# Gated DeltaNet layer on one core: when the output weight tiles are rounded in the even units

## The reference

```
h = rms_norm(x, norm_w) * (1 + scale) + shift            # scale, shift, gate from silu(c) @ ada_w + ada_b
p = h @ w_in                                             # 1024 x (q 1024, k 1024, v 2048, z 2048, b 8, a 8)
q, k, v = silu(causal_short_conv(q|k|v, conv_w))         # 4 taps
q, k = l2_norm(q) * 128**-0.5, l2_norm(k)
o = gated_delta_rule_chunked(q, k, v, sigmoid(b), g)     # 8 heads, key width 128, value width 256
o = rms_norm(o, norm_w) * silu(z)
x = x + gate * (o @ w_out)
out = rms_norm(x, final_norm_w)
```

## Time and profile before

| | us |
|---|---|
| median of 3 runs | 1266.35 |
| lowest and highest | 1266.05, 1270.23 |
| the profiled execution | 1268.89 |
| span of the profiled execution | 1267.1 |
| PE busy in the span | 1130.3 (89%) |
| DVE busy | 852.0 (67%) |
| POOL busy | 583.8 (46%) |
| ACT busy | 453.1 (36%) |

### The profile page before, as it was taken

The page is one execution under the profiler, slowest core; times in us unless marked ns, Lnnn a source line. Parts: engine busy times, 40 slices in busy tenths (PEclk is TensorE's granted clock), DMA queues, the critical chain, the costliest instruction groups (busy, mean ns, idle before and its releaser), DMA issues.

```text
span 1267.1 us, 19510 instructions
## 1 busy us (share of the span) xinstructions
PE 1130.3 (89%) x5628; PEld 921.6 (73%) x5628; DVE 852.0 (67%) x1896; ACT 453.1 (36%) x1038; POOL 583.8 (46%) x817
## 2 busy tenths in 40 slices
PE   2787699998999989998999989998999989998985
PEld 1665478777787878777787868877787868877763
DVE  3746668585857767585857767585758767585845
ACT  3452233424333332424333342434333432434323
POOL 3114454447444644447344644446344644446413
PEclk9888699999999999999999999999999999999988
DMA  9522331222222231222222231223122131213002
GB/s 302 168 84 76 89 92 38 61 55 67 63 51 51 62 76 38 59 54 76 54 49 52 63 76 38 60 53 84 45 59 54 50 76 45 66 40 92 21 34 117
DMA packets 150754, 88.31 MB, mean 70 GB/s; under 512 B 29446, under 2 KB 145320, under 8 KB 150696
## 3 DMA queue, kind: packets, MB, share of 16 engines
q1 hardware_dynamic: 150696, 87.73, 25.4%
HBM read 78.28 MB, written 9.44 MB: 69 GB/s over the span
## 4 chain that ended last, share of the span: by engine, by line
PE 54%; DVE 13%; POOL 13%; issue 13%; ACT 2%; DMA 2%; SPq 1%; DVEq 1%; POOLq 0%; ACTq 0%
PE bank L401 24%; PE bank L499 14%; POOL w_lo L1317 6%; DVE work L912 4%; POOL wo_lo L1324 3%; DVE y L945 3%; PE bank L545 2%; POOL w_raw L1331 2%; PE bank L459 2%; DMA work<-in_ada_w 2%; DVE gate_bc L1155 1%; PE bank L555 1%; PE bank L558 1%; PE bank L468 1%; PE bank L475 1%
## 5 line engine op out<-in xcount | busy, mean ns | idle before, releaser
L1317 POOL TENSOR_TENSOR w_lo<-w_raw,w_hi 128x256 fp32r<-128x256 f32 x384 | 316.8, 855 | 319.3 <-ACT w_hi L673 319.1
L401 PE MATMUL bank<-h_hi,w_hi 128*128 128x512 f32 x760 | 315.5, 415 | 28.7 <-POOL w_lo L1317 28.7
L401 PE MATMUL bank<-h_hi,w_lo 128*128 128x512 f32 x760 | 311.5, 410 | 0.0
L401 PE MATMUL bank<-h_lo,w_hi 128*128 128x512 f32 x760 | 310.5, 409 | 0.0
L401 PEld LDWEIGHTS bank<-h_hi,w_hi 128*128 128x128 f32 x760 | 144.9, 191 | 60.7 <-POOL w_lo L1317 33.1
L912 DVE SCALAR_TENSOR_TENSOR work<-pre,cw,work 128x512 f32<-128x512 f32 x192 | 173.1, 902 | 15.4 <-DVE work L909 5.4
L401 PEld LDWEIGHTS bank<-h_hi,w_lo 128*128 128x128 f32 x760 | 144.5, 190 | 30.2 <-issue 0.2
L401 PEld LDWEIGHTS bank<-h_lo,w_hi 128*128 128x128 f32 x760 | 144.8, 191 | 28.6
L1367 POOL TENSOR_TENSOR og_lo<-work,og_hi 128x256 fp32r<-128x256 f32 x64 | 47.1, 736 | 223.6 <-ACT og_hi L733 223.6
L699 ACT ACTIVATE work<-work 128x512 f32<-128x512 f32 x64 | 40.5, 633 | 300.3 <-DVE pre L920 143.2
L499 PE MATMUL bank<-wo_hi,og_hi 128*128 128x512 f32 x256 | 113.1, 442 | 16.3 <-DVE y L945 16.3
(11 more groups left out here) (174 smaller groups left out, 1897.3 us busy)
## 6 DMA issues: line engine op xcount, KB each, us to landing
w_raw<-in_gdn_w_in SPq DMA_DIRECT2D x96, 512.0 KB, 4.0
work<-in_ada_w SPq DMA_DIRECT2D x8, 1024.0 KB, 9.3
w_raw<-in_gdn_w_out SPq DMA_DIRECT2D x16, 512.0 KB, 3.3
y<-in_x SPq DMA_DIRECT2D x8, 512.0 KB, 8.1
work<-in_ada_w SPq DMA_DIRECT2D x8, 512.0 KB, 5.1
n_dram<-work SPq DMA_DIRECT2D x16, 256.0 KB, 4.5
out<-y SPq DMA_DIRECT2D x8, 512.0 KB, 2.7
t_dram<-work SPq DMA_DIRECT2D x16, 64.0 KB, 1.6
```

Of the source, the lines that this page charges most:

```text
L401: mm = nc.tensor.matmul(bank[m % 2][:, :], w[:, m % 2, k, :], h[:, k, half, :], start=(r == 0), stop=(r == MM - 1))
L1317: i = nc.gpsimd.tensor_tensor(w_lo[:, k % 2, j:j + 2, :], w_raw_k[:, k % 2, j:j + 2, :], w_hi[:, k % 2, j:j + 2, :].bitcast(F32), ALU.subt ...
```

## The change

In even units that have an output tile to prepare, three things change places. On ACT, the rounding of output tile 0 goes ahead of the tanh of k, and the rounding of output tile 1 goes ahead of the read-out of z (tile 1) and of the rounding of stream tile 3. On POOL, the low half of output tile 1 goes ahead of that of stream tile 3. No instruction is added or removed, and no wait.

```diff
@@ ACT, body(), not last @@
                     evacuate(u, 0)
                     split_hi(u, hd, par, 2)
-                    tanh(u, 0, 0, cvk[:, other, :])
                     if par == 0:
                         split_wo(hd, 0, u)
+                    tanh(u, 0, 0, cvk[:, other, :])
                     square(u + 1, "k", bank[6], k_ss)
                     decay_exp(u + 1)
+                    if par == 0:
+                        split_wo(hd, 1, u)
                     evacuate_z(u, 1, 0)
                     split_hi(u, hd, par, 3)
-                    if par == 0:
-                        split_wo(hd, 1, u)
@@ POOL, body(), not last @@
                     norm_k(u + 1)
                     mask_decay(u + 1)
-                    split_lo(u, 3)
                     if par == 0:
                         split_wo(hd, 1)
+                    split_lo(u, 3)
```

## The result

The changed kernel takes 1250.63 us (median of 4 runs, 1248.91 to 1251.62), the kernel before in the same comparison 1268.29 us (1266.05 to 1270.25). The ratio is 0.987 with a 95% interval of 0.9849 to 0.989. Two later comparisons on other occasions gave 0.9877 (0.9855 to 0.9899) and 0.9876 (0.9852 to 0.9899). The prediction said 1257.0 us, range 1250 to 1267: right in direction, inside the range near its low end, and 6.4 us too high. The gain within the comparison is 17.7 us; the forecast's own sum was 12.5 us less 0.6. The profiled execution has a span of 1247.9 us, 19.2 us less than before.

A forecast was written before the change was run, and what follows sets the result against it. PE was held by POOL's late low half of stream tile 4. Shorter waits (5.6 us, unit 0 0.6) and four clock falls gone (6.3) make 12.5 off 1268.89: 1256.4, plus 0.6 for a possible fall: 1257.0 us, range 1250 to 1267.

The forecast's parts named there:

- The wait moves from tile 4 to tile 3 and is shorter: PE's 2.8 us wait at stream tile 4 goes; a new 2.0 us wait comes at tile 3, 0.8 us shorter.
- The sign that I had given for it: PE idles 1.4 to 2.0 us at tile 3, directly after step `qs` of chunk 0, and not at tile 4.
- Its length: Tile 4 begins on PE at 457.4 instead of 458.20: 0.8 us per unit, 5.6 us over seven.
- by place: POOL's two groups keep their durations by position, not tile: first 2.84 us, second 3.25 us beside DVE's 128x512 gate.
- the fall that I had added: 0.6 us added to the forecast time for a clock fall that may come in one unit or other.
- The late gate of k: DVE's gate of k, beside POOL's subtraction of output tile 0, 0.5 to 0.6 us late; left out of the sum.
- The DMA of output tile 1 bounds the first part: POOL's gating of output tile 1 waits for its DMA until 438.06, so POOL gains 0.37 us, not 1.09.
- ACT's new wait: ACT waits for output tile 1's gating until 440.9; work behind is in time by 2 us or more, costing nothing.
- DVE's blocks: Blocks for DVE's row scheme, waited for 2.54 us before, are back at 453.4; DVE comes there at 456.4.
- The clock: PE's four clock falls go, 6.3 us, as the new 2.0 us wait is shorter than all that falls followed.

The follow-up runs named there:

- Output tile 1 alone: Changed kernel without its first part: output tile 0 is rounded behind the tanh of k, as before; 1259.92 us, ratio 0.9946 to the kernel before.
- the gate of k first: Changed kernel with POOL waiting, in even units, for DVE's gate of k before subtracting output tile 0; 1253.29 us, ratio 0.99 to the kernel before.
- the mask on DVE: Changed kernel with the masking of the decay matrix done by DVE instead of POOL; 1243.52 us, ratio 0.9819 to the kernel before; run again 1243.75 us.
- blocks late: Changed kernel with SP storing and reading back DVE's blocks behind stream tile 5's load in even units; 1251.25 us, ratio 0.9878 to the kernel before.

## Why the prediction was right, and where its size was off

**The wait moves from tile 4 to tile 3 and is shorter.** Right. No wait is left at tile 4, and the one at tile 3 follows step `qs` of chunk 0. Reordering POOL or ACT alone left the whole wait at one of the two tiles. The sign that I had given for it, 1.4 to 2.0 us idle at tile 3, fits one unit of eight only: the others show 0.85 us or less.

**Its length.** This term was mis-sized: I gained 0.8 us per unit, the profile shows 1.45 over units 4 to 14. Tile 3 came at 19.97 and not 20.33. The start of the gating cost 0.10 us more than I had, but the group that I gave 3.25 us took 2.81. I had kept durations "by place", because DVE's gate of z lies there, and had not carried on what I had worked out myself two paragraphs further: that the gate of k, and with it PE and the gate of z, would be 0.5 to 0.6 us late (it was 0.4), while POOL would be 0.4 us early (it was 0.3). The two slid apart just enough. Output tile 1 alone and the gate of k first both bring the 3.2 us back, and with it the loss. The margin is thin: 0.14 us less and the collision is there, as in unit 6. Another 0.16 us is in the way from tile 3 to tile 4, 7.79 us and not 7.95. A third of it is that I took 455.4 where 455.35 is nearer. The rest is the matmul directly behind two 256-column steps, which is followed after 0.42 us (447.45 before) where one that came later is followed after 0.34 us (445.00). The profile with the mask on DVE shows both: in its units 2 and 12 tile 3 came right behind step `qs`, was followed after 0.42 and 0.41 us, and tile 4 came 7.90 and 7.89 us later; in its five others after 0.33 to 0.36 us, and tile 4 after 7.79 to 7.83. With 0.13 us behind tile 4 this makes the 0.65 us per unit.

The profiled execution (1249.67 us) lies 7.3 us below the forecast. Of this 5.1 us are the seven units from unit 2 on, 0.4 us unit 0 (1.0 us gained, I had 0.6), and 0.6 us the fall that I had added. Another 0.9 us is that this execution reached unit 0 earlier, and 0.3 us lies behind unit 14; no experiment ties these two to the change. The median run is 1.0 us slower than the profiled one, which leaves 6.4.

**The late gate of k.** The Trainium skill (SBUF — State Buffer, Who interferes with whom) says that a DVE instruction with two SBUF inputs and a GpSimd instruction that reads SBUF exclude each other. The trace agrees: 0.69 us became 1.12 and the wait at the k transposes 1.31 instead of 0.89. POOL's group beside it took 3.23 us and not 2.80, which falls into its wait for the DMA. That the late gate costs nothing was right, and too modest: by the run with the gate of k first, being late was worth 3 us.

**The DMA of output tile 1 bounds the first part.** Right: 0.37 us of wait, 0.27 us gained where I had 0.37. But I valued the first part by this alone and by itself it makes 11 us, as it also moves the gate of z off POOL's last group and brings the waits down to where few clock falls follow.

**ACT's new wait.** Right: ACT waited 2.17 us for the gating and nothing behind it was late.

**DVE's blocks.** They were no part of the sum, as I had said that DVE comes there at 456.4, which is 27.3 us after ACT began stream tile 2; it was 27.2, without a wait. Delaying them cost nothing measurable, where my expectation had 4 us or more.

**The clock.** Four falls before, none in the units after: right in this profile, by 6.3 us. The reasons that I gave were not safe. The old waits were not near an edge: the same profile has 2.71 and 2.89 us in units 8 and 12, and no fall behind them. Nor is 2.0 us short enough: over the experiments falls came after idle times of 1.83, 1.93, 1.99 and 2.23 us. What saved the changed kernel is that its waits at tile 3 are 1.44 us or less (1.52 in its two other profiles). Its two of 1.8 and 2.0 us at the k transposes were lucky.

## What to carry to other kernels

When work shares one buffer and one serial engine, look for the piece that frees the buffer for the longest chain behind it, and put that first; the piece that it overtakes then has its own deadline, and the gain is the difference of the two waits. Change every engine of the chain at once: half of such a reordering was worth nothing here. And price contention by who asks when, not by the place in the program: shift one engine by 0.4 us and a 0.44 us collision can appear or vanish in each round, and here 0.14 us was enough in one unit.

## What the runs showed of the hardware

The granted clock of PE fell to 1.2 GHz for 3.4 us after single idle times inside otherwise dense work, beginning 0.1 to 1.5 us after the idle time's end. Between 180 and 1180 us the 14 profiles have 119 idle times of PE of 1.0 us or more, and 29 falls, each right behind one of them. None came behind the 72 idle times below 1.83 us, 10 behind the 20 from 1.83 to 2.02 us, and 19 behind the 27 from 2.23 to 2.89 us. So one idle time doesn't tell whether the clock falls: 1.97, 2.58 and 2.89 us passed without one in some units. These are counts from this kernel, not a rule; in the last unit, where PE idles more, falls also came behind 1.75 us.

A fall behind the wait at tile 3 or 4 costs 1.5 to 1.6 us here. Behind the k transposes it costs 1.1 us (with blocks late: 43.59 us from ACT's stream tile 2 to the state step of chunk 3 in unit 4, 42.46 in unit 6), as it takes the place of the wait at tile 3.

Kernels with waits of this size therefore differ from run to run by some falls. The same kernel, with the mask on DVE, ranged from 1240.91 to 1248.92 us over six runs; its three longest had a mean granted clock of 0.970 to 0.971, its three shortest 0.975 to 0.978.

POOL's group of four 128x256 subtractions takes 2.8 us alone. It takes 3.2 to 3.3 us if a 128x512 gate of DVE, with both inputs in SBUF, is asked for before its last piece, and 2.8 us if during it.
